# A longer ring for finished tiles, and another order at the mixer's entry

## The reference

```
h  = rmsnorm(x, norm1_w) * (1 + sc1) + sh1
z  = h @ w_in + b_in                          # RG-LRU half and mLSTM half
x1 = x + g1 * (concat(y_lru, y_mlstm) @ w_out)
h2 = rmsnorm(x1, norm2_w) * (1 + sc2) + sh2
y  = rmsnorm(x1 + g2 * peer(h2), final_norm_w)

peer: for each token and each of 8 heads
  q = h2 @ wq, normalised, two halves of 128
  top 16 of q1.k1 and of q2.k2, top 16 of their 256 sums -> 16 experts of 16384
  out += sum_k softmax_k * gelu(u[expert_k] . h2) * v[expert_k]
```

## Time and profile before

| | us |
|---|---|
| Median of 3 runs | 3336.39 (3335.85 to 3336.85) |
| Profiled execution, device time | 3336.33 |
| Its span, first to last instruction | 3334.4 |
| First gather's issue, in the span | 597.29 |
| Last gather's landing, in the span | 3321.44 |

### The profile page before, as it was taken

How to read it: one execution, slowest core, us unless ns; L and a number is a source line. 1 busy time by engine, 2 the same in 40 slices (tenths; PEclk the granted TensorE clock), 3 DMA queues, 4 the chain that set the end, 5 groups by cost and what they waited for, 6 DMA issues and landing times. The chain is left out here.

```text
span 3334.4 us, 38191 instructions
## 1 busy us (share of the span) xinstructions
PE 2878.8 (86%) x9454; PEld 1410.0 (42%) x9454; DVE 2226.7 (67%) x5472; ACT 2153.0 (65%) x7214; POOL 1203.7 (36%) x1134
## 2 busy tenths in 40 slices
PE   7999999788888888888888888888888888888886
PEld 5665455444434443443344334333444344434331
DVE  5687265667676667666766676667666766676665
ACT  3332143477776777777777777777777777777775
POOL 0000110344444444444444444444444444444443
PEclk9999999899999999999999999999999999999999
DMA  7231132899999999999999999999999999999998
GB/s 282 86 112 66 33 117 90 353 419 411 419 419 407 410 419 416 404 416 419 416 401 420 419 416 399 419 420 406 406 419 419 415 396 419 420 418 397 419 420 328
DMA packets 170094, 1191.19 MB, mean 357 GB/s; under 512 B 20042, under 2 KB 21482, under 8 KB 30226
## 3 DMA queue, kind: packets, MB, share of 16 engines
q0 software_dynamic: 155792, 1118.53, 81.7%
q1 hardware_dynamic: 14084, 70.23, 5.8%
HBM read 1179.42 MB, written 9.25 MB: 356 GB/s over the span
## 5 line engine op out<-in xcount | busy, mean ns | idle before, releaser
L911 PE MATMUL ps<-r_w,r_yT 128*128 128x512 f32 (+1 forms) x3168 | 1525.9, 615 | 330.1 <-ACT r_yT L1236 323.0
L1805 DVE SCALAR_TENSOR_TENSOR r_yT<-r_w,r_qk 128x1024 bf16<-128x1024 f32 x792 | 969.9, 1226 | 692.6 <-DMA r_w<-in_peer_uv,gidx 692.3
L584 POOL DMA_INDIRECT r_w<-in_peer_uv,gidx x792 | 864.9, 1092 | 1024.6 <-PE ps L911 923.8
L911 PEld LDWEIGHTS ps<-r_w,r_yT 128*128 128x128 f32 (+1 forms) x3168 | 553.4, 189 | 1217.2 <-issue 1214.4
L911 PE MATMUL ps<-r_yT 128*128 128x512 f32 (+1 forms) x1056 | 518.5, 624 | 79.7 <-ACT r_yT L1236 78.0
L1228 ACT ACTIVATE mixc<-mixc 128x1 f32<-128x1 f32 x1056 | 207.7, 197 | 481.3 <-DVE r_yT L1805 480.5
L584 POOL DMA_INDIRECT r_yT<-in_peer_uv,gidx x264 | 296.4, 1123 | 542.1 <-PE ps L911 445.6
L1236 ACT ACTIVATE r_yT<-ident,mixc 128x128 f32<-128x128 f32 x1024 | 411.0, 401 | 33.4
L1232 ACT ACTIVATE mixc<-mixc 128x1 f32<-128x1 f32 x1056 | 409.3, 388 | 35.0
L1231 ACT ACTIVATE mixc<-mixc 128x1 f32<-128x1 f32 x1056 | 408.3, 387 | 33.8
L1805 DVE SCALAR_TENSOR_TENSOR r_yT<-r_yT,r_qk 128x1024 bf16<-128x1024 f32 x264 | 323.4, 1226 | 112.4 <-DMA r_yT<-in_peer_uv,gidx 107.5
(11 more groups left out here) (287 smaller groups left out, 2312.1 us busy)
## 6 DMA issues: line engine op xcount, KB each, us to landing
r_w<-in_ada_w SPq DMA_DIRECT2D x18, 1024.0 KB, 5.3
r_w<-in_peer_uv,gidx POOLq DMA_INDIRECT x792, 13.9
r_w<-in_w_lin SPq DMA_DIRECT2D x16, 512.0 KB, 8.3
r_yT<-in_peer_uv,gidx POOLq DMA_INDIRECT x264, 11.9
r_vo<-in_x_prompt SPq DMA_DIRECT2D x8, 512.0 KB, 6.7
r_qk<-in_ada_w SPq DMA_DIRECT2D x2, 2048.0 KB, 16.3
r_w<-in_w_out SPq DMA_DIRECT2D x2, 2048.0 KB, 8.5
r_w<-in_x_prompt SPq DMA_DIRECT2D x8, 512.0 KB, 3.5
```

What stands on the lines that cost most here:

```text
L584: pool.indirect_dma_start(ring[place(h, j)], None, table, bass.IndirectOffsetOnAxis(gidx_t[:, h, j:j + 1], 0))\
L911: mm = nc.tensor.matmul(ps[0:r, 2 * p + c, :], diag[:, j % 4, 0:r], row[:, D + c * 512:D + (c + 1) * 512], start=h == 0 and j == 0, stop=h ...
L1805: V.scalar_tensor_tensor(udump[j % 2], ring[i][:, 0:D], 1.0, h2[:, t, :], ALU.mult, ALU.mult, accum_out=dots[:, i:i + 1]).then_inc(dot_don ...
```

## The change

- Ring: `PLACES` = 11. The first 8 are as before, but those of w_out's first half (c = 0) are now 0 and 1, `r_yT`'s are 2 and 3, w_out's second half 4 and 5. Place 8 + i lies in `h2` of tiles 2i and 2i + 1 and joins at slot `slot0(2i + 2, 1) + 12`, after a wait on the stores of tiles 0 to 2i + 1 (`y_st`). Which place a slot takes is computed ahead, first in, first out.
- Entry, Pool: it waits for 17 projections before gather 0, for the 18th before gather 2, and stores the last x1 before gather 4.
- Entry, SP: head 4 of peer_wq and the final norm's row are loaded with heads 2 and 3, head 5 after 16 projections; heads 6 and 7 and g2 stay.
- Entry, PE, ACT and DVE: another order, below.
- g1 of the prompt (`g1p`) lies in two separate pieces, loaded by two DMAs, and the sample's g2 in another tile's part of `h2`.
- The increments for which nobody waits go.

```diff
+PLACES = 11
-        g1p, sh2b, a2b = hT[:, 3:5, 484:996], hT[:, 5:7, 484:996], r_wr[:, :]
+        g1p, sh2b, a2b = (r_hT[:, 4708:5220], r_hT[:, 7872:8384]), hT[:, 5:7, 484:996], r_wr[:, :]
-        ring = [r_yT[:, i * 2048:(i + 1) * 2048] for i in range(2)] + [
-            r_w[:, 4096 + i * 2048:6144 + i * 2048] for i in range(4)] + [r_w[:, i * 2048:(i + 1) * 2048] for i in range(2)]
+        ring = [r_w[:, 4096 + i * 2048:6144 + i * 2048] for i in range(2)] + [r_yT[:, i * 2048:(i + 1) * 2048] for i in range(2)] + [
+            r_w[:, 8192 + i * 2048:10240 + i * 2048] for i in range(2)] + [r_w[:, i * 2048:(i + 1) * 2048] for i in range(2)] + [
+            r_qk[:, i * 2048:(i + 1) * 2048] for i in range(PLACES - RING)]
...
+        def joins(i):
+            return 2 * i + 2, slot0(2 * i + 2, 1) + 12
+        place, uses, last_use = [], [], []
+        free = [(i - RING, i) for i in range(RING)]
+        turns = [0] * PLACES
+        for n in range(N_SLOTS):
+            free += [(n - PLACES, RING + i) for i in range(PLACES - RING) if joins(i)[1] == n]
+            used, i = free.pop(0) if free[-1][1] < RING or turns[free[-1][1]] else free.pop()
+            place.append(i)
+            last_use.append(used)
+            turns[i] += 1
+            uses.append(turns[i])
+            free.append((n, i))
...
@@ SP @@
+            load_wq(4)
+            sp.dma_start(fwb, A["final_norm_w"].partition_broadcast(P)).then_inc(g2_ld, 16)
+            sp.wait_ge(o_mm, 2 * NT - 2)
+            load_wq(5)
             sp.wait_ge(o_mm, 2 * NT)
             sp.wait_ge(h2_ready, NT)
-            for h in range(4, HEADS):
-                load_wq(h)
+            load_wq(6)
+            load_wq(7)
...
@@ Pool @@
-            pool.wait_ge(o_mm, 2 * NT)
+            pool.wait_ge(o_mm, 2 * NT - 1)
...
-                        pool.wait_ge(v_free, slot0(t, h) + (j + 1))
+                        n = slot0(t, h) + j
+                        i = place[n]
+                        if uses[n] > 1 or i < RING:
+                            pool.wait_ge(v_free, RING + last_use[n] + 1)
+                        else:
+                            pool.wait_ge(y_st, 16 * joins(i - RING)[0])
+                        if t == 0 and h == 0 and j == 2:
+                            pool.wait_ge(o_mm, 2 * NT)
+                        if t == 0 and h == 0 and j == 4:
+                            store_x1(NT - 1)
                         if t == 0 and h == 0 and j == 6:
-                            store_x1(NT - 1)
...
-                        pool.sem_inc(pool_turn, 1)
...
@@ PE, where project() now takes the range of k @@
-            project(NT - 2, 0)
             pe.wait_ge(o_ev, 2 * (NT - 3) + 2)
             turn(0, 0, P)
+            project(NT - 2, 0)
             turn(0, 1, P)
-            pe.wait_ge(p_ready, NT)
-            project(NT - 2, 1)
+            turn_y(NT - 1)
             pe.wait_ge(nd_done, NT)
             query(0, 0, 0)
-            turn_y(NT - 1)
+            pe.wait_ge(p_ready, NT)
+            project(NT - 2, 1, range(4))
             pe.wait_ge(o_ev, 2 * (NT - 2) + 1)
             scores(0, 0)
+            project(NT - 2, 1, range(4, KD))
             project(NT - 1, 0)
             project(NT - 1, 1)
             query(0, 1, 0)
...
@@ ACT @@
+            turned_y(NT - 1)
             query(0, 0)
-            turned_y(NT - 1)
             norm(0)
-            query(0, 1)
+            softmax(0)
             x1_norm(NT - 2)
             x1_root(NT - 2)
-            softmax(0)
             x1_norm(NT - 1)
             x1_root(NT - 1)
-            norm(1)
-            turned_sample()
+            query(0, 1)
...
+                        if t == 0 and h == 0 and j == 1:
+                            norm(1)
+                            turned_sample()
...
@@ DVE @@
             projected(NT - 2, 0)
+            route(0)
             projected(NT - 2, 1)
             residual(NT - 2)
-            route(0)
             projected(NT - 1, 0)
+            scaled(NT - 2)
+            gates(0, 0)
             projected(NT - 1, 1)
             residual(NT - 1)
-            scaled(NT - 2)
-            gates(0, 0)
-            scaled(NT - 1)
...
                     dot(t, h, 0)
                     dot(t, h, 1)
+                    if t == 0 and h == 0:
+                        scaled(NT - 1)
+                        route(1)
                     dot(t, h, 2)
                     dot(t, h, 3)
-                    if t == 0 and h == 0:
-                        route(1)
```

More of the change, by code:

```diff
@@ L162, in build @@
         qrt, qrs, nsv0, psm, prs, fss, frs = (work(1) for _ in range(7))
-        dots = mixc[:, 0:RING]
-        sq, kd, gd, th, wc = (mixc[:, RING + 2 * i:RING + 2 * i + 2] for i in range(5))
+        dots = mixc[:, 0:PLACES]
+        sq, kd, gd, th, wc = (mixc[:, PLACES + 2 * i:PLACES + 2 * i + 2] for i in range(5))
         gidx_t = gidx[:, :].rearrange("p (h j) -> p h j", h=HEADS)
@@ L261, in build @@
         wq_ld = [sem(f"wq_ld{h}") for h in range(HEADS)]
-        e_ld = [sem(f"e_ld{j}") for j in range(RING)]
+        e_ld = [sem(f"e_ld{j}") for j in range(PLACES)]
         dot_done, dg_ready, v_free, acc_free = (sem(n) for n in ("dot_done", "dg_ready", "v_free", "acc_free"))
@@ L548, in _ @@
             mod_rows(g1s, 2, 1, P, bc_ld)
-            mod_rows(g1p, 2, 0, P, bc_ld)
+            for c in range(2):
+                pool.dma_start(g1p[c], mod_dram[0, 2 * D + c * 512:2 * D + (c + 1) * 512].partition_broadcast(P)).then_inc(bc_ld, 16)
             mod_rows(a2b, 4, 1, DEC, bc_ld)
@@ L582, in tile @@
                             pool.wait_ge(x1_st[2], 48)
-                        pool.sem_inc(pool_turn, 1)
-                        pool.indirect_dma_start(ring[place(h, j)], None, table,
-                                                bass.IndirectOffsetOnAxis(gidx_t[:, h, j:j + 1], 0))\
-                            .then_inc(e_ld[place(h, j)], 16)
+                        pool.indirect_dma_start(ring[i], None, table,
+                                                bass.IndirectOffsetOnAxis(gidx_t[:, h, j:j + 1], 0)).then_inc(e_ld[i], 16)
             each_tile(tile)
@@ L805, in turn_y, with project @@
                 m.then_inc(y_tr, 1)
-            def project(i, c):
+            def project(i, c, ks=range(KD)):
                 t = ORDER[i]
@@ L826, in project @@
                     pe.wait_ge(o_ev, max(2 * i - 1 + c, 2))
-                for k in range(KD):
+                for k in ks:
                     y = yT[:, k, t * P:t * P + r] if k < 4 else yTB[i % 2][:, k - 4, 0:r]
@@ L830, in project @@
                                          start=k == 0, stop=k == KD - 1)
-                m.then_inc(o_mm, 1)
+                if k == KD - 1:
+                    m.then_inc(o_mm, 1)
             turn_keys(0)
@@ L907, in mix @@
                 pe.wait_ge(dg_ready, slot0(t, h) + (j + 1))
-                pe.sem_inc(pe_turn, 1)
-                row = ring[place(h, j)]
+                row = ring[place[slot0(t, h) + j]]
                 for c in range(2):
@@ L1225, in weight @@
                 wch.base, wch.n = s * K_W, 0
-                i, d = j % 2, dots[:, place(h, j):place(h, j) + 1]
+                i, d = j % 2, dots[:, place[s]:place[s] + 1]
                 act.wait_ge(dot_done, s + 1)
@@ L1629, in projected @@
                 r = rows(t)
-                g1 = g1s if t == NT - 1 else g1p
                 if i == 0 and c == 0:
-                    dve.wait_ge(bc_ld, 64)
+                    dve.wait_ge(bc_ld, 80)
                 dve.wait_ge(o_mm, 2 * i + c + 1)
@@ L1640, in projected @@
                     return
-                V.tensor_tensor(h2[0:r, t, c * 512:(c + 1) * 512], ps[0:r, project_bank(i, c), :], g1[0:r, c, :],
+                V.tensor_tensor(h2[0:r, t, c * 512:(c + 1) * 512], ps[0:r, project_bank(i, c), :], g1p[c][0:r, :],
                                 ALU.mult).then_inc(o_ev, 1)
@@ L1709, in best_scores @@
                 dve.wait_ge(r_mm, m + 2)
-                hold()
                 V.max(top[:, lo[0]], sc[:, s2[0]])
@@ L1800, in dot @@
                 s = slot0(t, h) + j
-                i = place(h, j)
-                dve.wait_ge(e_ld[i], landed(t, h, j))
+                i = place[s]
+                dve.wait_ge(e_ld[i], 16 * uses[s])
                 if s >= 2:
```

13 lines of the change are left out of this document (2 added, 11 removed).

## The result

The changed kernel takes 3313.51 us (median of 6 runs, 3311.17 to 3315.66), the kernel before 3336.78 beside it (6 runs, 3335.85 to 3339.32). The ratio is 0.9931 [0.9918, 0.9943]: **23 us faster**, 19 to 27. Forecast were 15, with 3321 us and a range of 3307 to 3331; the narrower "own range" of 3315 to 3327 was missed by 1.5 us. The gain at the entry came by the steps that were forecast, and one term of the sum, the increments, was three times too small.

A forecast was written before the change was run, and what follows sets the result against it. The mixer was taken as bound by its DMA stream of 1056 gathers. Gains of 5.9 + 6.2 - 1 (entry) + 2 (ring) + 2 (increments) = 15.1 us took 3336.3 to 3321 us, range 3307 to 3331, own range 3315 to 3327.

The forecast's parts named there:

- the increments: Turn increments on Pool, PE and DVE: removing some 2600 instructions gives between 0 and 4 us, 2 taken.
- The first gather: Entry, chain to the first gather: it goes at about 591.4 instead of 597.29, 5.9 us sooner.
- The moved bytes: Entry: 2.62 MB of loads move to the idle DMA time before the first gather, 6.2 us less in the stream.
- What is late next: Entry, behind the first gathers: gather 10 goes at about 624.5, 626 being the latest without cost; up to 4 us, 1 taken.
- rival B: Entry's gain is eaten: route(1) starves the stream, gather 10 goes 6 to 10 us later, 3329 to 3331; chance 0.16.
- The entry's 11.1 us: Entry in all: 5.9 us from the first gather plus 6.2 from moved bytes, less 1 for late work.
- The ring: Places 9, 10 and 11 in tiles 2, 4 and 6 give 2 us, with ends 0 and 21.
- Rival A: Holes in the mean DMA share are real time; the ring fills those of tiles 2 to 7, 19 us more, 3302; chance 0.10.
- The tile periods: Sign: tiles 2 to 7 within 1 us of before; over 1.5 us means wrong, tiles 4 to 7 over 2 shorter proves real holes.
- deeper queues buy nothing: Ring: if one trailing DMA part sets the landings, deeper queues buy nothing; by the mean share they would buy 21 us.
- the same recurring shift: Sign in the gathers' landings: distance stays 2.49 us, with the 0.9 to 1.0 us shift every 20 to 22 gathers unchanged.
- Rival C: More gathers in flight slow the landings' rhythm; at +0.03 us per gather from slot 284 on, 3344 us; chance 0.05.

The follow-up runs named there:

- e_after8: The changed kernel with a ring of 8 places throughout, the increments still gone; 3317.28 us, ratio 0.9940 to the kernel before.
- e_entry: The changed kernel with 8 places throughout and all increments put back, so only the new entry; 3322.63 us, ratio 0.9957 to the kernel before.
- e_ring: The kernel before with the ring growing to 11 places, increments kept on three older semaphores, the sample's g2 moved; 3333.01 us, ratio 0.9990.
- e_turns: The kernel before without the increments for which nobody waits on Pool, PE and DVE, nothing else changed; 3329.61 us, ratio 0.9982.
- e_sp: The kernel before with 2560 more increments on SP, 320 behind each of the first eight stores of a finished tile; 3335.78 us, ratio 1.0000.
- e_pool_four: The kernel before with four Pool increments behind each gather instead of one ahead of it; 3334.41 us, ratio 0.9998.
- e_ring6: The changed kernel with six ring places throughout, ACT kept three mixes ahead; 3414.09 us, ratio 1.0226 to the kernel before.
- e_t_pool: The kernel before without Pool's increment ahead of each gather, PE's and DVE's kept; 3333.50 us, ratio 0.9991.

## Why the prediction was right, and where not

**The first gather: right.** Forecast about 591.4; e_after8 and e_entry have 590.95 and 590.78. In after's profile it is 588.33, with the whole trunk 2.6 us earlier than in e_after8's. The steps before it hold too: routing from 577.97 in e_entry (577.9 forecast), then projected and residual of tile 7, the x1 store at 589.82 (589.8 forecast), the gather; two gathers go before the third may. As the trunk's end moves by up to 2.6 us between profiles, an agreement to within 0.6 us is in part luck.

**The moved bytes: right.** Forecast 6.2 us; putting them back costs 5.5, and 6.1 by the landing.

**What is late next: right, and rival B false.** Gather 10 was forecast for 624.5 and goes at 619.72 (622.33 in e_after8). The piece that was feared is there: best_sums waits 2.53 us for ACT's norm, and PE, idle for 7.91 us before it, then mixes slot 2 in 3.78 us while the granted clock from 612 to 620 is 0.50, the lower level (1.2 GHz), against 1.99 us for the mix at 605.77. The row of PE's timeline:

```profile
615.66 3.78 PE L930 MATMUL ps<-r_yT 128*128 128x512 f32 x4 [7.91 <-ACT r_yT L1256]
```

But ten gathers were queued, and loads and stores worth 8.7 us by the forecast's estimate, and the DMA stayed full. Slot 10 lands at 633.4 to 634.3 in e_after8 and e_entry, with 8 places and the moved loads; slot 9 at 631 plus one gather was forecast. The entry's 11.1 us were 10.9 by the landing. By the medians they are 14, with 11.1 inside the interval; e_entry's profile, its slowest run, can't tell the two apart.

**The ring: the size nearly right, the picture only in part.** 2 us were forecast, 3.3 and 3.8 measured. Rival A forecast 19 us more and is false by the medians of e_ring and e_after8. The tile periods, which were to tell it apart, did so badly: tiles 4 to 7 take 325.9, 327.2, 326.8 and 326.5 us against 328.3, 328.1, 327.9 and 328.8 before, so two of them are over 2 us shorter, past the 1.5 us named as a sign of being wrong. But in e_turns, with 8 places, they are 326.5, 327.4, 327.7 and 328.1: against these the ring has 3.3 us in four tiles, and the rest is the increments'. The text also took it that by bytes the holes would nearly vanish with 11 places, and they did not. From 3025 to 3039 the share is 0.68 at 266 GB/s, by bytes (421 - 266) x 14 / 421 = 5.2 us, deeper than the 0.79 to 0.95 before. Yet from 3022.06 to 3036.96 six gathers land in 14.90 us, 2.483 each, no shift at all. The added places let the leading parts run further ahead and then stand still for longer; only the trailing one sets a landing. At the end it is 11 us behind instead of 5. Whether these are always the same engines no view tells. The sixteen increments of each gather show more than the mean: in after the last two come 0.31 us apart (median) and the fourteenth 5.3 us ahead of them, 8.0 us from 2690 on, so it is two parts that trail there. The Trainium skill's page "DMA: Bandwidth & Descriptors", section "Latency and other measured facts", says that engines 7 and 15 are usually slower than the others in traces. Two trailing parts agree with it in number, but which engines they are is not shown here. The prediction took from that rule that deeper queues buy nothing; the 3.3 us (0.3 to 6.3) of e_ring and the 3.8 of e_after8 stand against this in its strict form.

**The increments: the step that failed.** "Between 0 and 4 I take 2" was mis-sized: 6.0 us measured in the kernel before and 5.4 in the changed one. "On the landings' rhythm the engines' issue has no part, 0" is neither borne out nor refuted, as the intervals of the runs on Pool's increment reach to nothing. The reason given for the 2, that instruction packets share the DMA engines, is half right: the shift does come behind packets of queue 14, but SP's and Pool's cost nothing (e_sp, e_pool_four), so the share of all instructions, 7%, was the wrong measure. The forecast of "the same recurring shift" failed with it: it falls from 0.97 to 0.61 in after, and to 0.60 to 0.69 in all kernels with 8 or more places that have none of the increments, and in no other of these (e_ring6, with 6 places, has 0.86). That is where the trace shows the gain: from slot 10 to the last, 2676.3 us before and 2671.1 in e_turns. (Slot 10 lands 3 us sooner as well, but 2 of these are there at the store of tile 7's x1 already, and the trunk moves by that much between profiles.) The idle time ahead of Pool's gathers that is put down to its own issue falls from 180 us to 55 at the same time, but it falls to 45 in e_t_pool and to 44 in e_pool_four as well, so it is not the gain. Which engine's increments give it, and by which way, stays open: single engines moved the time by 1 to 3 us each, within their intervals. Pairs of engines were not tried.

**Rival C is false**: eleven gathers in flight land every 2.49 us, 3286.57 to 3296.51 being 9.94 us for four gathers.

So the total was 8 us off: 4 from the increments, 1 to 2 from the ring, and up to 3 from the entry, which the landings don't confirm. That 3313.5 lies inside the range is in part luck: below 3315 the range was made for rival A, which is false. The chances don't follow from their own terms either: 0.69 + 0.10 and half of 0.16 are 0.87 for faster, and 0.08 is left for same, where 0.85 and 0.10 stand.

## What to carry to other kernels

Where a stream of large gathers is the bound, read its progress from the landings of what waits for it, at two slots far apart, and not from the mean share of the DMA engines: a hole in the mean costs nothing while the slowest part has work queued. Then start the stream sooner, and put other loads into the silence before it; both paid what the rows said, to within 1 us by the landings, closer than two profiles can tell. Deepen the queue until the longest gap in issue is covered, here 8 places, and expect little from more; and price bare semaphore increments in the steps of a loop by taking them all out once, since the rows of the profile don't show their cost.

## What the runs showed that was not expected

The lag of the trailing part behind the mean share grows with the queue: 5 us with 8 places (before), 8 and 11 with 11 (e_ring, after), and in after two parts trail together. Removing all bare increments on Pool, PE and DVE, some 2600, gave 6 us, while adding 2560 on SP cost 0 ± 3 us. And the shift of 0.97 us that comes back every 20 to 22 gathers mostly follows, by about 2 us, an 8 KB packet of instructions on queue 14; with 8 places or more it shrinks to 0.6 to 0.7 only where all three engines have lost their increments.
